# Statistics of queries and keys: two fp32r matmuls with a GpSimd remainder in place of one float32 matmul

## What is computed

```python
def _rms(x, w):
    x32 = x.astype(jnp.float32)
    y = x32 * lax.rsqrt(jnp.mean(x32 * x32, axis=-1, keepdims=True) + EPS)
    return (y * w.astype(jnp.float32)).astype(x.dtype)
...
q, k, v, cb, cc, cx, pu = jnp.split(u @ w_in, COL_SPLITS, axis=-1)
q = _apply_rope(_rms(q.reshape(B, S, H, 2, dh), q_norm_w), cos, sin)
k = _apply_rope(_rms(k.reshape(B, S, H, 2, dh), k_norm_w), cos, sin)
```

## Time and profile before

| | us |
|---|---|
| median of 3 runs | 1755.82 (1755.58 to 1755.90) |
| the profiled execution | 1756.91 |
| its span | 1755.1 |
| TensorE busy | 1687.6 (96%) |
| VectorE busy | 1082.3 (62%) |
| ScalarE busy | 613.9 (35%) |
| GpSimd busy | 79.3 (5%) |
| granted TensorE clock, mean | 0.988 |

### The profile page before, as it was taken

One profiled execution on the slowest core, in us unless ns is written; L12 is line 12 of the kernel. 1 busy time (PEld: TensorE's weight loads), 2 busy tenths in 40 slices (PEclk: granted clock), 3 DMA queues, 4 the chain that ended last, 5 costly groups with the idle time before them and its releaser, 6 DMA issues.

```text
span 1755.1 us, 24815 instructions
## 1 busy us (share of the span) xinstructions
PE 1687.6 (96%) x8955; PEld 1405.1 (80%) x8955; DVE 1082.3 (62%) x1642; ACT 613.9 (35%) x909; POOL 79.3 (5%) x144
## 2 busy tenths in 40 slices
PE   3999999999998999999999999999999999899999
PEld 1888888887785778888888878888888788589999
DVE  2877777436558667777753277777423376665554
ACT  3422222124525543222222252222222363554443
POOL 0000000000001000000000000000000000000000
PEclk9999999999999999999999999999999999999999
DMA  9466555422221025655552226665323324045554
GB/s 369 135 190 192 183 189 180 144 96 68 89 96 48 25 72 180 188 186 183 188 168 96 97 97 191 183 187 183 107 96 96 96 87 138 17 144 180 183 185 149
DMA packets 69719, 249.23 MB, mean 142 GB/s; under 512 B 7424, under 2 KB 8448, under 8 KB 69504
## 3 DMA queue, kind: packets, MB, share of 16 engines
q1 hardware_dynamic: 51200, 180.83, 32.2%
q0 software_dynamic: 18432, 67.12, 12.0%
HBM read 246.87 MB, written 1.05 MB: 141 GB/s over the span
## 4 chain that ended last, share of the span: by engine, by line
PE 90%; DVE 6%; ACT 2%; SPq 1%; issue 1%; DMA 1%; DVEq 0%; ACTq 0%
PE ps L1007 29%; PE ps L1008 28%; PE ps L1009 28%; PE ps L1058 1%; DVE shared_b L720 1%; PE ps L1192 1%; DMA raw<-wstream 1%; DVE wlo L609 1%; DVE nmax L905 1%; PE ps L1219 1%; DVE xl L706 1%; SPq L280 1%; ACT prob L511 1%; PE ps L1144 0%; ACT whi L349 0%
## 5 line engine op out<-in xcount | busy, mean ns | idle before, releaser
L609 DVE TENSOR_TENSOR wlo<-raw,whi 128x1024 fp32r<-128x1024 f32 x320 | 392.0, 1225 | 585.3 <-ACT whi L349 583.4
L1007 PE MATMUL ps<-xh,whi 128*128 128x512 f32 (+1 forms) x1880 | 682.4, 363 | 23.4 <-DVE xl L706 18.3
L349 ACT ACTIVATE whi<-raw 128x1024 fp32r<-128x1024 f32 x320 | 339.6, 1061 | 1022.8 <-PE ps L1009 1006.2
L1008 PE MATMUL ps<-xl,whi 128*128 128x512 f32 (+1 forms) x1880 | 665.3, 354 | 0.0
L1009 PE MATMUL ps<-xh,wlo 128*128 128x512 f32 (+1 forms) x1880 | 664.4, 353 | 0.0
L1007 PEld LDWEIGHTS ps<-xh,whi 128*128 128x128 f32 x1880 | 359.5, 191 | 87.6 <-issue 31.0
L1008 PEld LDWEIGHTS ps<-xl,whi 128*128 128x128 f32 x1880 | 361.0, 192 | 48.8 <-issue 3.8
L1009 PEld LDWEIGHTS ps<-xh,wlo 128*128 128x128 f32 x1880 | 360.6, 192 | 47.6
L634 DVE SCALAR_TENSOR_TENSOR shared_a<-wm,cs,shared_a 128x512 f32<-128x512 f32 x448 | 307.6, 748 | 0.0
L1007 PE MATMUL ps<-ah,whi 128*128 128x512 f32 (+1 forms) x704 | 255.9, 364 | 0.0
L1008 PE MATMUL ps<-al,whi 128*128 128x512 f32 (+1 forms) x704 | 255.4, 363 | 0.0
(11 more groups left out here) (109 smaller groups left out, 818.2 us busy)
## 6 DMA issues: line engine op xcount, KB each, us to landing
raw<-wstream SPq DMA_DIRECT2D x320, 512.0 KB, 3.5
wm<-wmod POOLq DMA_DIRECT2D x128, 512.0 KB, 3.7
wm<-wmod SPq DMA_DIRECT2D x3, 2048.0 KB, 20.8
h<-x_t SPq DMA_DIRECT2D x1, 2048.0 KB, 11.7
wm<-wmod SPq DMA_DIRECT2D x2, 1024.0 KB, 20.5
K<-cols SPq DMA_DIRECT2D x1, 1195.0 KB, 14.4
out_t<-h SPq DMA_DIRECT2D x8, 128.0 KB, 2.5
K<-cols SPq DMA_DIRECT2D x1, 268.5 KB, 2.9
```

The lines of the kernel that those rows point to most:

```text
L349: act.activation(whi[:, n % SPL, :, :].rearrange("p a b -> p (a b)"), raw[:, s, :], ACT.Copy)\
L609: dve.tensor_tensor(wlo[:, n % SPL, :, :].rearrange("p a b -> p (a b)"), raw[:, n % RAW, :], whi[:, n % SPL, :, :].rearrange("p a b -> p ( ...
L1007: pe.matmul(out_ap, hi_w, hi_x, start=start, stop=False)
L1008: pe.matmul(out_ap, hi_w, lo_x, start=False, stop=False)
```

## The change

Each query or key block's squares become two fp32r tiles. ScalarE's square of the bank goes to `sqh`, in fp32r, which rounds it. GpSimd squares `kq[:, b]` (the copy in SBUF) in float32 into `sqk`, waits for itself, and subtracts `sqh` from it into `sql`, also fp32r. TensorE's statistic waits for `sql_done` and is two fp32r matmuls, of `sqh` and of `sql`, with an fp32r copy of `halves` that ScalarE makes once at the start of the first mixer. The two tiles lie where `prob` and what follows it stand; those are written later.

GpSimd's loop `square_low(l)` stands behind the loads that end in the feed-forward stages before, and ahead of `query_zeros(l)`.

```diff
+            def square_low(l):
+
+                for b in range(QKB):
+                    wb = T if b < 4 else ntile(l)
+
+                    pool.wait_ge(sqh_done, 8 * l + b + 1)
+                    if b >= 2:
+                        pool.wait_ge(qk_stat, 8 * l + b - 1)
+                    pool.tensor_tensor(sqk[:, b % 2, 0:wb], kq[:, b, 0:wb], kq[:, b, 0:wb], ALU.mult)\
+                        .then_inc(sqk_done, 1)
+                    pool.wait_ge(sqk_done, 8 * l + b + 1)
+                    pool.tensor_tensor(sql[:, b % 2, 0:wb], sqk[:, b % 2, 0:wb],
+                                       sqh[:, b % 2, 0:wb].bitcast(F32), ALU.subtract).then_inc(sql_done, 1)
+
             after_mix = (LATE_UNIT + 1) * PAIRS // 2 + 1
             loads(u0 // 2 + 1, after_mix)
+            square_low(0)
             query_zeros(0)
             conv_pool_low(0)
             loads(after_mix, UNITS * PAIRS // 2)
+            square_low(1)
             query_zeros(1)
             conv_pool_low(1)
...
                 n0, w = B_win[l], ntile(l)
+                if l == 0:
+                    act.activation(halves[:, :], col("halves", 0, P), ACT.Copy).then_inc(halves_done, 1)
...
-                        act.activation(sqk[:, b % 2, 0:wid(b)], ps[:, b % 4, 0:wid(b)], ACT.Square)\
-                            .then_inc(sqk_done, 1)
+                        act.activation(sqh[:, b % 2, 0:wid(b)], ps[:, b % 4, 0:wid(b)], ACT.Square)\
+                            .then_inc(sqh_done, 1)
...
+                if l == 0:
+                    pe.wait_ge(halves_done, 1)
                 def stat(b):
 
                     qk, wb = 8 * l + b, T if b < 4 else w
-                    pe.wait_ge(sqk_done, qk + 1)
+                    pe.wait_ge(sql_done, qk + 1)
                     if b >= 2:
                         pe.wait_ge(rq_done, qk - 1)
-                    pe.matmul(ps[:, 6 + b % 2, 0:wb], col("halves", 0, P), sqk[:, b % 2, 0:wb], start=True, stop=True)\
+                    pe.matmul(ps[:, 6 + b % 2, 0:wb], halves[:, :], sqh[:, b % 2, 0:wb], start=True, stop=False)
+                    pe.matmul(ps[:, 6 + b % 2, 0:wb], halves[:, :], sql[:, b % 2, 0:wb], start=False, stop=True)\
                         .then_inc(qk_stat, 1)
...
-                            pe.wait_ge(sqk_done, 8 * l + b - 3)
+                            pe.wait_ge(sqh_done, 8 * l + b - 3)
```

More of the change, by code:

```diff
@@ L111, in program @@
         mrows = sb("mrows", [P, P])
+        halves = sb("halves", [P, P], F32R)
         lamt = sb("lamt", [P, 2, DH])
@@ L140, in program @@
         rot = sb("rot", [P, S])
+        squares = ExitStack()
+        sqh = squares.enter_context(nc.sbuf_tensor("sqh", [P, 2, T], F32R))
+        sql = squares.enter_context(nc.sbuf_tensor("sql", [P, 2, T], F32R))
+        squares.close()
         prob = sb("prob", [P, 2, 2, T])
@@ L198, in program @@
         evac = sem("evac")
+        halves_done = sem("halves_done")
+        sqh_done = sem("sqh_done")
         sqk_done = sem("sqk_done")
+        sql_done = sem("sql_done")
         qk_stat = sem("qk_stat")
```

## The result

The changed kernel takes 1769.6 us (six runs, 1769.35 to 1772.17) against 1755.75 for the kernel before. The ratio is 1.0082, 95% interval 1.0069 to 1.0095: 14 us slower, where 6.5 were forecast. The direction was right, the time lies outside the range.

A forecast was written before the change was run, and what follows sets the result against it. TensorE was taken to bound the kernel, with the port shared by VectorE and GpSimd taking over in layer 1's query blocks. Layer 0's -1.0 and layer 1's +7.5 gave +6.5 us, a median of 1762.3, range 1756.5 to 1766.5.

The forecast's parts named there:

- The copy of `halves`: ScalarE's new copy in mixer 0: hidden in ScalarE's idle 2.45 us, so nothing; without cover about 0.2 us.
- the forecast of the rest: The whole predicted sum, in which the copy counted nothing: -1.0 in layer 0 and +7.5 in layer 1, +6.5 us.
- TensorE's saving: Statistics of both mixers: two fp32r matmuls for one fp32 save 0.43 on each of twelve wide ones, 5.2 us; narrow ones nothing.
- GpSimd's operations: Square and subtraction between ScalarE's square and the statistic: each 1.26 us at 512 columns, 0.72 at 256.
- The assumed hand-overs: Delays between dependent operations around GpSimd: 0.08 us from ScalarE, 0.09 to itself, 0.12 to TensorE.
- Start of each stage: First statistic of each mixer: TensorE waits for the GpSimd pair, 2.35 us late in each layer, together 4.7.
- The fourth statistic of layer 1: Last key block of layer 1: TensorE waits for GpSimd behind VectorE's port use, 2.56 us late.
- the order at the port: Fourth statistic of layer 1: VectorE's rope goes first with 0.79 us, then GpSimd's subtraction.
- The query blocks: Layer 1's four narrow blocks: port load of 4.24 us a block against a period of 3.29, 4.3 us lost in all.
- Rival 1, the clock: TensorE's pauses at three places bring lower clock: 1.7 us per loss, one giving +8.2, 1764.0 us; chance 0.17.
- signs of being wrong: In the changed profile: query blocks 3.3 apart, no first-statistic pause, GpSimd operations far from 1.26, or clock below 1.00.
- Rivals 2 to 4: Both mixers: waits without port, +1.0, chance 0.12; all GpSimd work hidden, 1750.6, 0.06; cheap multiply with lock, +3.0, 0.05.

The follow-up runs named there:

- E2: The kernel before plus only ScalarE's copy of `halves`, read by nobody, and TensorE's wait for it ahead of the first blocks; 1765.46 us, 1.0050.
- E1: The changed kernel with TensorE's wait for `halves` put behind the mixer's first two blocks instead of ahead of them; 1761.87 us, 1.0030.
- E3: As E1 without GpSimd's loops and the remainder: both fp32r matmuls take the rounded squares, with `halves` at half value; 1752.87 us, 0.9971.
- E4: As E1, but each GpSimd operation is a memset of scratch of the same length, waits kept, remainder left out; 1757.31 us, 1.0007.
- E6: As E1, but only blocks 1 to 7 of layer 0 and 1 and 2 of layer 1 take the new form; 1753.84 us, 0.9974.
- E8: As E1, but each statistic is one fp32r matmul of the rounded squares, without remainder or GpSimd work; 1748.81 us, 0.9956.

## Why the prediction was right or wrong

**The copy of `halves`: wrong, and as much as the whole error.** The step read "ScalarE, which then sits idle 2.45 us before its next split: nothing; without this cover it would be one small activation, about 0.2 us". The cover was true for ScalarE: the activation of 0.29 lies in its idle time. The step priced the operation and not the wait on it. It never asked where TensorE's wait stands and what is queued behind it: the matmuls of the first two blocks, which had run beside the normalisation. Measured: 8.35 us in the trace, 8.9 (E2) and 7.7 (the change against E1) in the medians. Kept apart, the forecast of the rest, +6.5, stands against E1's +5.3 by the ratio, within its interval of 3.2 to 7.2.

**TensorE's saving: right at each statistic.** 0.43 a 512-wide statistic was forecast, 0.39 to 0.44 measured, 5.1 in all (E3). The narrow ones gain nothing while VectorE repeats every 3.28. The prediction did not follow this one step further: TensorE's lead from the wide statistics of layer 1 is partly lost at the same limit, 0.77 in E3.

**GpSimd's operations: near.** The square took 1.10 and 0.61 rather than 1.26 and 0.72 (up to 0.80 in the narrow blocks, beside VectorE), the subtraction 1.27 and 0.80 to 0.97. The assumed hand-overs of 0.08, 0.09 and 0.12 are 0.08, 0.09 and 0.05 at layer 1's first statistic.

**Start of each stage: right in kind.** The statistic was to come 2.35 late. The splits moved by 1.71 + 0.43 = 2.1 in layer 0: the forecast less 0.16 for the square and 0.07 for the hand-over to TensorE.

**The fourth statistic of layer 1: a third less than forecast.** It was to be 2.56 late (its own times, 1434.7 less 1432.09, give 2.6); the splits say 1.26 + 0.43 = 1.7. The step that failed is the order at the port: VectorE's rope was to go ahead of GpSimd's subtraction. With the shorter square, GpSimd was ready first (1442.27 against 1442.28), and VectorE's scaling waited instead, 1.81 in place of 0.75.

**The query blocks: right in mechanism, above in size.** 4.3 forecast, 3.2 measured, 3.1 of it taken away by E4. The rule of "SBUF — State Buffer", section "Who interferes with whom", in the Trainium skill holds here on both sides: GpSimd's reading operations stretch VectorE's two-input rows (from 0.42 to 0.84, from 0.75 to 1.81), and its writing ones leave them at 0.48 and 0.75 (E4).

**Rival 1, the clock: it came, once in the change.** It was given 0.17 and 1.7 us; the stretch in layer 1 costs 3.31 - 1.71 = 1.6. In E1 it came in both layers. A clock below 1.00 in these stages is also among the prediction's own signs of being wrong. It made up for the port's smaller share, so the sum of 6.5 met E1's span of 6.4 with errors that cancel. By stage the changed kernel has -1.3 us in layer 0, where -1.0 was forecast, and +6.9 in layer 1 for +7.5, of which 1.6 is the clock: without it the stages of layer 1 cost 5.3.

**Rivals 2 to 4.** Without a port the sum was +1.0; E4, which is that case on the chip, gives +0.7 by the medians. In its splits layer 0 gives -1.3 for -1.2, and layer 1 +3.7 with one stretch at the lower clock, so 2.1 without it, for +2.2. The cover held at nine of the twelve wide statistics, as forecast, and not at the three that this rival needed; the multiply was not cheap.

What stays open is why 1.90 us of pause left the clock alone in one place and 1.81 did not in another, and why the stretch at the lower clock behind one and the same normalisation differs from kernel to kernel. These differences, 1.2 us a place, lie in every comparison of two traces here, so a single step of the splits is a firmer number than a difference of two spans.

## What to carry to other kernels

A constant that is prepared once must be ready before the first wait on it can hold anything: put its making at a place where its engine is early, and put the wait directly ahead of the instruction that reads it. A split into rounded part and remainder pays on TensorE only where a whole matmul block hides the remainder's chain; take it there and leave the rest alone (E6). Ahead of a stage that another engine limits, part of what TensorE saves is lost again (0.77 of 5.05 in E3). Before work is moved to GpSimd, add its reading time to VectorE's two-input time in each period: where the sum exceeds the period, both are late.

## What the runs showed of the hardware

- A GpSimd multiply of a tile with itself takes 1.10 us for 128x512, the subtraction of two tiles 1.27.
- Pauses of TensorE of 1.8 to 1.9 us can be followed by a stretch at the lower clock level, 1.6 us lost (eight of ten), or by none (two). One of 1.50 was followed by such a stretch in E8 and not in the kernel before.
- Behind one and the same wait of 2.97 us TensorE was back at the full clock in the changed kernel (1.00 over 658 to 662) where the kernel before was not (0.63 over 651 to 655), 1.2 us in the time.
- A GpSimd memset of 1.28 us beside VectorE's two-input scaling leaves it at 0.75; a subtraction of 1.27 that starts 0.01 ahead makes it 1.81.
- The profile names one releaser in each row. Where TensorE passed two waits, the matmul's row has the 13.4 us against VectorE, which had long been done; the row of the weight load ahead of it has them, as 14.3, against the copy that ended last.
